# Retention head norm: the sums of squares as two fp32r products of a split tile, the split made on GpSimd

## What is computed

```python
def head_rmsnorm(o):
    return o * lax.rsqrt(jnp.mean(o * o, axis=-1, keepdims=True) + NORM_EPS)

def mixer_merge(o_ret, g, conv_b, conv_c, conv_x, gate_ret, gate_conv, conv_w, w_ret_out, w_conv_out, w_out):
    b, h, n, dv = o_ret.shape
    o = head_rmsnorm(o_ret).transpose(0, 2, 1, 3).reshape(b, n, h * dv).astype(g.dtype)
    y_ret = (jax.nn.silu(g) * o) @ w_ret_out
...
```

## Time and profile before

| what | us |
|---|---|
| median of 3 runs | 2120.68 (2120.48 to 2120.81) |
| the profiled execution, its time | 2120.12 |
| the profiled execution, its span (first to last instruction) | 2118.3 |
| PE busy in the span | 2109.1 |
| DVE busy | 1432.8 |
| ACT busy | 803.6 |
| POOL busy (four small memsets at the start) | 0.2 |

### The profile page before, as it was taken

The page is one execution under the profiler, slowest core; times in us unless marked ns, Lnnn a source line. Parts: engine busy times, 40 slices in busy tenths (PEclk is TensorE's granted clock), DMA queues, the critical chain, the costliest instruction groups (busy, mean ns, idle before and its releaser), DMA issues.

```text
span 2118.3 us, 25984 instructions
## 1 busy us (share of the span) xinstructions
PE 2109.1 (100%) x10483; PEld 1785.1 (84%) x10483; DVE 1432.8 (68%) x1976; ACT 803.6 (38%) x1196; POOL 0.2 (0%) x4
## 2 busy tenths in 40 slices
PE   9999999999999999999999999999999999999998
PEld 7888888988888888898888888888888898888887
DVE  5677777668588773577777767733335689777765
ACT  5322222456322222342222233222223565557654
POOL 0000000000000000000000000000000000000000
PEclk9999999999999999999999999999999999999999
DMA  8655555431555543355555544433333446775664
GB/s 271 211 176 159 170 163 157 136 93 41 159 151 159 182 149 96 90 150 169 175 164 161 171 135 148 131 99 100 92 95 112 130 120 199 208 209 153 189 191 145
DMA packets 452412, 318.12 MB, mean 150 GB/s; under 512 B 10543, under 2 KB 427719, under 8 KB 451911
## 3 DMA queue, kind: packets, MB, share of 16 engines
q1 hardware_dynamic: 430492, 243.43, 40.0%
q10 hardware_dynamic: 21800, 73.03, 10.4%
HBM read 312.23 MB, written 1.05 MB: 148 GB/s over the span
## 4 chain that ended last, share of the span: by engine, by line
PE 99%; DMA 1%; DVE 0%; SPq 0%; ACT 0%; issue 0%; DVEq 0%
PE bank L661 22%; PE bank L662 22%; PE bank L663 22%; PE bank L672 9%; PE bank L675 5%; PE bank L1005 4%; PE bank L709 2%; PE bank L749 1%; PE bank L768 1%; PE bank L767 1%; PE bank L769 1%; PE bank L713 1%; PE bank L753 1%; DMA WM<-in_w_mod_dram 1%; PE bank L1049 0%; PE bank L1050 0%
## 5 line engine op out<-in xcount | busy, mean ns | idle before, releaser
L1623 DVE TENSOR_TENSOR LO<-RAW,HI 128x1024 fp32r<-128x1024 f32 (+1 forms) x431 | 518.2, 1207 | 334.3 <-ACT HI L1149 334.1
L661 PE MATMUL bank<-Y,HI 128*128 128x512 f32 (+1 forms) x1416 | 551.1, 389 | 0.0
L663 PE MATMUL bank<-Y,LO 128*128 128x512 f32 (+1 forms) x1416 | 549.3, 388 | 0.0
L662 PE MATMUL bank<-Y,HI 128*128 128x512 f32 (+1 forms) x1416 | 549.2, 388 | 0.0
L1149 ACT ACTIVATE HI<-RAW 128x1024 fp32r<-128x1024 f32 (+1 forms) x431 | 437.2, 1039 | 143.7 <-DMA RAW<-in_w_in_dram 52.8
L663 PEld LDWEIGHTS bank<-Y,LO 128*128 128x128 f32 x1416 | 265.9, 188 | 54.7
L661 PEld LDWEIGHTS bank<-Y,HI 128*128 128x128 f32 x1416 | 265.9, 188 | 54.5 <-issue 0.5
L662 PEld LDWEIGHTS bank<-Y,HI 128*128 128x128 f32 x1416 | 265.9, 188 | 54.3 <-issue 0.5
L1634 DVE SCALAR_TENSOR_TENSOR MODACC<-MODRAW,SC,MODACC 128x1024 f32<-128x1024 f32 x224 | 277.3, 1280 | 3.2 <-DMA MODRAW<-in_w_mod_dram 2.8
L1348 ACT ACTIVATE TMP<-bank 128x512 f32<-128x512 f32 x66 | 39.5, 598 | 454.0 <-PE bank L663 373.4
L672 PE MATMUL bank<-Y,HI 128*128 128x512 f32 x720 | 181.0, 393 | 0.0
(11 more groups left out here) (294 smaller groups left out, 2538.8 us busy)
## 6 DMA issues: line engine op xcount, KB each, us to landing
RAW<-in_ffn_w_up_dram SPq DMA_DIRECT2D x170, 512.0 KB, 3.9
MODRAW<-in_w_mod_dram ACTq DMA_DIRECT2D x128, 512.0 KB, 4.4
RAW<-in_w_in_dram SPq DMA_DIRECT2D x128, 512.0 KB, 4.1
RAW<-in_ffn_w_down_dram SPq DMA_DIRECT2D x66, 512.0 KB, 3.9
RAW<-in_ffn_w_down_dram SPq DMA_DIRECT2D x24, 384.0 KB, 3.4
WM<-in_w_mod_dram SPq DMA_DIRECT2D x16, 512.0 KB, 9.0
RAW<-in_w_ret_out_dram SPq DMA_DIRECT2D x16, 512.0 KB, 4.2
RAW<-in_w_conv_out_dram SPq DMA_DIRECT2D x16, 512.0 KB, 4.0
```

The lines of the kernel that those rows point to most:

```text
L661: mm(bank, hi, X[:, k, 0, cols], start=first, stop=False)
L662: mm(bank, hi, X[:, k, 1, cols], start=False, stop=False)
L663: return mm(bank, lo, X[:, k, 0, cols], start=False, stop=end)
L1623: V_.tensor_tensor(weights(v, 1), raw_weights(v), weights(v, 0).bitcast(F32), ALU.subtract).then_inc(lo_done, 1)
```

## The change

The fp32 product of each head becomes two fp32r products. GpSimd gets a block of its own. It rounds the ones once (`ONESR`). Then, for each of the eight heads (four in each layer), it copies the tile of sums to `HSH` as fp32r, which rounds it, and subtracts the rounded tile from the whole into `HSL`. PE multiplies `ONESR` with `HSH` and adds the product of `ONESR` with `HSL` in the same bank. `HSH` lies where `SQACC` lies and `HSL` where `CV` lies, both unused in this stage; `ONESR` is new memory.

```diff
+    HSH = place("HSH", [P, 512], F32R, cursor[0])
     SQACC = place("SQACC", [P, 512])
     RB = place("RB", [P, 512])
+    HSL = place("HSL", [P, 512], F32R, cursor[0])
     CV = place("CV", [P, 512])
+    ONESR = place("ONESR", [P, P], F32R)
...
                     def head_sumsq(h):
-                        pe.wait_ge(osum_done, s.hh + h + 1)
                         bank_wait(pe, s.hs[h])
-                        mm(B[s.hs[h].bank][:, 0:T], ONES[:], TMP[:, 2 * (h % 2), 0:T], start=True, stop=True
-                           ).then_inc(hss_done, 1)
+                        pe.wait_ge(ones_rounded, 1)
+                        pe.wait_ge(head_hi, s.hh + h + 1)
+                        mm(B[s.hs[h].bank][:, 0:T], ONESR[:], HSH[:, 0:T], start=True, stop=False)
+                        pe.wait_ge(head_lo, s.hh + h + 1)
+                        mm(B[s.hs[h].bank][:, 0:T], ONESR[:], HSL[:, 0:T], start=False, stop=True).then_inc(hss_done, 1)
...
+        @block.gpsimd
+        def _(pool):
+            pool.wait_ge(small_set, 1)
+            nc.gpsimd.tensor_copy(ONESR[:], ONES[:]).then_inc(ones_rounded, 1)
+            for s in stages:
+                if s.kind != "ret":
+                    continue
+                for h in range(HEADS):
+                    n = s.hh + h
+                    t = TMP[:, 2 * (h % 2), 0:s.T]
+                    pool.wait_ge(osum_done, n + 1)
+                    if n:
+                        pool.wait_ge(hss_done, n)
+                    nc.gpsimd.tensor_copy(HSH[:, 0:s.T], t).then_inc(head_hi, 1)
+                    pool.wait_ge(head_hi, n + 1)
+                    nc.gpsimd.tensor_tensor(HSL[:, 0:s.T], t, HSH[:, 0:s.T].bitcast(F32), ALU.subtract).then_inc(head_lo, 1)
```

More of the change, by code:

```diff
@@ L448, in build @@
         hss_done, hrb_done = sem("hss_done"), sem("hrb_done")
+        ones_rounded, head_hi, head_lo = sem("ones_rounded"), sem("head_hi"), sem("head_lo")
         half_row_done, half_scaled, half_base_done = (
```

## The result

The changed kernel takes 2125.68 us (median of 12, 2124.01 to 2126.97), the kernel before 2120.58 (median of 12, 2120.14 to 2120.89): +5.1 us, a ratio of 1.0023 with an interval of 1.0016 to 1.0031. It is slower, by little more than can be told. The prediction was 2129.7 with a range from 2125.0 to 2133.5, so the time lies in the range, near its low end. The profiled execution is one of the slower ones, 2126.40 us, with a span of 2124.6.

The account below looks back on a forecast made before the run. PE, busy in 100% of the span, was taken as the bound. Head 0 +6.1, clock +2.2, head 2 +1.0, head 3 -0.4 and layer 1 +0.1 gave +9.0 us: 2129.7, range 2125.0 to 2133.5.

Parts of the forecast that it names:

- its own signs of being wrong: Prediction wrong if the first GpSimd subtraction follows its copy like the others, or DVE's subtractions at 491 to 500 lengthen or separate.
- no cost of the library: Rival: the library instruction ahead of GpSimd's first subtraction costs nothing at its place; +0.7 us, 2121.4, chance 0.15.
- the contention: Rival: DVE and GpSimd take turns at layer 0's head 1, DVE's chain slips 2.3 us, total 2132.0; chance 0.13.
- The library instruction: Layer 0, head 0: loading the subtraction's code after GpSimd's first copy takes 6.3 us, with ends of 1.3 and 9.0.
- Head 0: Layer 0's first head: PE waits for GpSimd's copy, library load and subtraction, and finishes the product 6.1 us later.
- GpSimd's two instructions: Copy and subtraction per head: 1.05 and 1.22 us at 512 elements, 2.6 with hand-overs; 1.6 in all at 256.
- The fall of the clock: After PE's 6.5 us wait at layer 0's head 0, its clock halves for scores(3), adding 2.2 us.
- Head 2: Layer 0: DVE's sum ends in its own time, GpSimd's rest comes 2.6 us later, PE's product finishes 1.0 us later.
- the 0.4 saved at head 1: Layer 0, head 1: no wait for GpSimd, so PE's cheaper products save 0.4 us, lost again at head 2.
- Head 3: Layer 0: the rest is ready at 513.5 before PE comes at 513.8, so no wait and 0.4 us saved.
- Layer 1: Its four heads: heads 0 and 1 save 0.2 us each, lost at head 3; +0.1 us in all.
- The ceiling of 2.4 us: PE's work saved at all eight heads by replacing fp32 products with fp32r ones, the most possible gain: 2118.3 us, 0.11% faster.

Follow-up runs that it names:

- e1: Changed kernel with the ones rounded at the start by a GpSimd tensor_tensor, moving the library instruction there; 2124.95 us, ratio 1.0021 to the kernel before.
- e2: Changed kernel with VectorE's sums of heads 0 and 1 moved behind its subtractions in both layers; 2123.64 us, ratio 1.0012 to the kernel before.
- e5: Changed kernel, but head 2 of layer 0 keeps the fp32 product and GpSimd skips that head; 2124.21 us, ratio 1.0016 to the kernel before.
- e7: Changed kernel with layer 0's sums behind subtractions and PE's head products later (layer 0 heads 0 to 2, layer 1 head 0); 2121.80 us, ratio 1.0005.
- e10: The changed kernel measured once more, unaltered, on one chip with the kernel before; 2125.55 us, ratio 1.0024; its profiled execution took 2124.01 us.
- e3: Changed kernel without the split: both fp32r products take one rounded tile, GpSimd has no such work; 2119.27 us, ratio 0.9992 to the kernel before.
- e8: As the changed kernel with later PE products, plus layer 0 head 3's products moved into the next stage's second unit; 2120.76 us, ratio 0.9998.

## Why the prediction was right, and where it was wrong

The direction, slower, and the range held, but the sum of +9.0 was made of the wrong terms: the load and the clock behind it, 8.3 of the 9.0 us, are not there, and about 3 us of other costs, with what comes and goes from execution to execution, stand in their place. That the time lies in the range is luck. By its own signs of being wrong the prediction was wrong: the first subtraction follows its copy like the others, and VectorE's subtractions get longer than 0.69 us. Two rivals came true together, no cost of the library (+0.7) and the contention (+2.3); I had not added them up, to 2123.7.

- **The library instruction, +6.3, was wrong.** The step "it can't begin before about 492, and the first subtraction stands behind it" put a price on it from the load of a tile and a table. It costs nothing: 0.08 us between copy and subtraction, with it (changed kernel) or without (e1), and nothing ahead of the first such instruction when it stands at the start (e1). The rule of the Trainium skill (GPSIMD Engine Reference, 2.1 Instruction dispatch) about some 6 us at a first call does not show in these traces. Head 0 cost 1.05 us instead of 6.1, with a copy of 2.21 us in it where one alone takes 0.61.
- **GpSimd's two instructions were mis-sized, and that by a little.** By themselves they take 0.61 and 1.27 us where I took 1.05 and 1.22 (at 256 elements 0.40 and 0.73 where I took 0.63 and 0.69); from the end of the sum (508.15) to PE's second product (510.23) it is 2.1 us, not 2.6. The subtraction is 1.85 times VectorE's 0.69; the 1.96 of the Trainium skill (GPSIMD Engine Reference, 3. Performance versus the Vector engine), for an addition, is near.
- **The contention, a rival with 0.13, was right in kind.** It was priced at 2.3 us and costs 1.4 of VectorE's chain at head 1, and, which I had not seen, 1.6 us of GpSimd's own copy at head 0. What the Trainium skill says (SBUF — State Buffer, SBUF: two separate sides), one engine holding the shared ports for a whole instruction, agrees with the 1.78 us of one VectorE subtraction beside GpSimd, against 0.69 alone: it ends 0.55 us after GpSimd's subtraction. At head 0 the copy is kept for longer than one instruction: it is on record from 492.05, 0.15 us after the first of VectorE's three subtractions starts, and ends behind all three. What removing the contention alone is worth is not measured: e2's 2.0 us have the missing fall of the clock in them.
- **The fall of the clock was right in kind and wrong in place.** I had +2.2 behind a wait of 6.5 us at head 0; it came behind head 2, in some executions only, and costs 1.58 us. That a wait must be as long as the 4 to 5 us at the span's end was read from one place and was wrong: here PE waits 1.57 and 0.78 us with one product between.
- **Head 2, +1.0, was mis-sized.** Mine had the 0.4 saved at head 1 in it; counted so, it is 2.5 - 0.4 = +2.1: 0.7 of the wait that I had, and 1.4 of VectorE's slip, which I had only as a rival. The reason that I gave, that VectorE gets there in its own time whatever PE has saved, is what e5 and e7 show again at head 3, where the wait comes as soon as PE gets there early.
- **Head 3, -0.4,** is -0.4. **Layer 1, +0.1,** is +0.45 through its heads, partly because GpSimd is slowed at heads 0 and 1 there as well (a copy of 0.79 us for 0.40, a subtraction of 1.27 for 0.73). Behind them come +1.3 by the load of a weight tile in the first profile, and nothing in e10.
- **The ceiling of 2.4 us held**, and was still too high: 1.5 us with no split at all (e3), because part of what PE saves is waited for again, 0.24 us in layer 1's stage and 0.40 behind its heads in e3's profile.

In order: 0.2 (start) + 1.05 - 0.4 + 2.5 + 1.6 - 0.4 + 0.45 + 1.3 = 6.3 us, the difference of the two profiled executions' spans. For e10, the same program, it is 0.7 (start) + 1.05 - 0.4 + 2.5 - 0.4 + 0.45 = 3.9, again the difference of the spans (2122.2 against 2118.3). What both have is 3.2 us, and that is the change's own; the clock (1.6), the load (1.3) and the start (0.2 to 0.7) come and go, and the medians, with a mixture of them, are 5.1 apart.

## What to carry to other kernels

Ask of a cheaper product what makes its operands, and where: here PE's 2.4 us were bought with 16 us on GpSimd, which held VectorE's subtractions up and was held up by them, and PE's waits for the split, 3.3 us with the delay of VectorE's chain in them, were larger than the gain. Put GpSimd's work beside VectorE work that it does not meet (here the reciprocal, which has one input tile, the only such instruction tried), not beside subtractions of two tiles in SBUF. Two waits close together can also be followed by a fall of PE's clock; with idle products in them it was not seen to fall, but moving the waiting product later in PE's order (e8) removes the waits themselves and brings the time back to the kernel's before. And before a wait is charged to a change, look for it in a second profile of the same program.

## What I had not expected of the hardware

PE's granted clock fell after waits of 1.57 and 0.78 us with one product between them, in one profiled execution and in that of e1, and not in e10 with the same waits; the cost was 1.58 us and the low level lasted 3.4 us. GpSimd's first use of a library instruction cost no time that the trace or the median shows. A GpSimd copy of 512 elements, 0.61 us alone, took 2.21 us beside three VectorE subtractions in a row and ended 0.5 us after the last of them. At head 1 it starts as long after the first of them (499.71, 0.15 us behind 499.56) and the two take turns: 1.01 and 1.61 us for GpSimd, 1.78 for VectorE's last. Why the same order of starts goes one way at head 0 and the other at head 1 no run here shows. The load of one weight tile took at most 4.5 us in one execution and 6.2 in another of the same program, measured from the unit's end to ACT's start.
